# A hybrid attention and recurrent layer on one core: weights as the stationary operand for the columns of the recurrent branch

## The reference

```
h    = rms_norm(x) * norm_w * (1 + scale) + shift      # scale, shift from silu(c) @ w_ada
proj = h @ w_in                                        # q | k | v | z_a | f | x_r | z_r
att  = forgetting_attention(q, k, v, f)                # 16 heads of 128
y_a  = (att * silu(z_a)) @ w_br_attn
xc   = causal_conv4(x_r) + conv_b                      # per channel, over tokens
r, i = sigmoid(xc_block @ w_rg_a + b), sigmoid(xc_block @ w_rg_x + b)   # 16 blocks of 128
a    = exp(-8 * r * softplus(-lru_lambda))
hr_t = a_t * hr_(t-1) + sqrt(1 - a_t^2) * (i_t * xc_t) # a scan over tokens
y_r  = (hr * silu(z_r)) @ w_br_rnn
g    = sigmoid(h @ w_gate + b_gate)                    # g_a | g_r
y    = x + gate_res * ((g_a * y_a + g_r * y_r) @ w_out)
```

## Time and profile before

| | |
|---|---|
| median of three runs | 2623.95 us (2623.81 to 2624.01) |
| the profiled execution's own time | 2624.72 us |
| its span, first to last instruction | 2622.9 us |
| PE busy (matmuls) | 2579.7 us, 98% of the span |
| PEld busy (weight loads) | 2138.8 us, 82% |
| DVE, ACT, POOL busy | 73%, 47%, 1% |
| granted TensorE clock, mean | 0.997 of full |
| DMA | 266 GB/s on average |

### The profile page before, as it was taken

One profiled execution on the slowest core, in us unless ns is written; L12 is line 12 of the kernel. 1 busy time (PEld: TensorE's weight loads), 2 busy tenths in 40 slices (PEclk: granted clock), 3 DMA queues, 4 the chain that ended last, 5 costly groups with the idle time before them and its releaser, 6 DMA issues.

```text
span 2622.9 us, 30908 instructions
## 1 busy us (share of the span) xinstructions
PE 2579.7 (98%) x11668; PEld 2138.8 (82%) x11668; DVE 1906.0 (73%) x1885; ACT 1231.7 (47%) x1436; POOL 18.1 (1%) x32
## 2 busy tenths in 40 slices
PE   4999999999999999999999999999999999999999
PEld 4888888888888888888888888888888888888887
DVE  6889999899888566665666666668787878754544
ACT  4554333433343466654566555554444444433333
POOL 0000000000000000000000000000000000000000
PEclk8999999999999999999999999999999999999999
DMA  9999999999998566445666666679998989667675
GB/s 373 345 333 348 326 356 337 338 351 335 347 343 290 168 195 185 131 143 163 197 194 198 198 198 198 197 268 356 311 352 312 351 312 350 215 209 225 210 225 173
DMA packets 351128, 698.77 MB, mean 266 GB/s; under 512 B 26338, under 2 KB 30724, under 8 KB 350724
## 3 DMA queue, kind: packets, MB, share of 16 engines
q1 hardware_dynamic: 350608, 696.69, 79.3%
q10 hardware_dynamic: 372, 0.12, 0.0%
HBM read 692.45 MB, written 4.19 MB: 266 GB/s over the span
## 4 chain that ended last, share of the span: by engine, by line
PE 97%; DMA 1%; DVE 1%; issue 0%; ACT 0%; SPq 0%; DVEq 0%; ACTq 0%
PE ps_acc L1110 31%; PE ps_acc L1112 31%; PE ps_acc L1118 31%; DMA ada_first<-in_w_ada 1%; PE ps_t L1192 1%; PE ps_t L1237 1%; PE ps_c L1158 0%; DVE acc L743 0%; PE ps_t L1190 0%; PE ps_t L1229 0%; PE ps_t L1181 0%; PE ps_t L1246 0%; PE ps_c L1200 0%; PE ps_t L1272 0%; PE ps_d L1209 0%
## 5 line engine op out<-in xcount | busy, mean ns | idle before, releaser
L539 ACT ACTIVATE w_hi<-land 128x1024 fp32r<-128x1024 f32 x896 | 950.6, 1061 | 1301.4 <-PE ps_acc L1112 1059.8
L726 DVE TENSOR_TENSOR w_lo<-land,w_hi 128x1024 fp32r<-128x1024 f32 x896 | 1094.2, 1222 | 634.0 <-ACT w_hi L539 633.5
L1110 PE MATMUL ps_acc<-w_hi,h_hi 128*128 128x512 f32 x3068 | 1203.8, 392 | 0.0
L1112 PE MATMUL ps_acc<-w_hi,h_lo 128*128 128x512 f32 x3068 | 1195.3, 390 | 0.0
L1118 PE MATMUL ps_acc<-w_lo,h_hi 128*128 128x512 f32 x3068 | 821.0, 389 | 0.0
L1118 PEld LDWEIGHTS ps_acc<-w_lo,h_hi 128*128 128x128 f32 x3068 | 575.6, 188 | 121.7 <-DVE w_lo L726 1.3
L1112 PEld LDWEIGHTS ps_acc<-w_hi,h_lo 128*128 128x128 f32 x3068 | 576.6, 188 | 118.9
L1110 PEld LDWEIGHTS ps_acc<-w_hi,h_hi 128*128 128x128 f32 x3068 | 576.6, 188 | 118.7
L743 DVE SCALAR_TENSOR_TENSOR acc<-ada_ring,cvec,acc 128x1024 f32<-128x1024 f32 x217 | 277.4, 1279 | 4.1 <-DMA ada_ring<-in_w_ada 3.8
L1008 DVE SCALAR_TENSOR_TENSOR racc<-res_land,cvec,racc 128x1024 f32<-128x1024 f32 x124 | 158.6, 1279 | 0.4 <-DMA res_land<-in_w_ada 0.4
L861 DVE TENSOR_TENSOR store<-ps_acc,store 128x1024 f32<-128x1024 f32 x89 | 108.5, 1219 | 13.1 <-PE ps_acc L1118 12.9
(11 more groups left out here) (200 smaller groups left out, 1042.2 us busy)
## 6 DMA issues: line engine op xcount, KB each, us to landing
land<-in_w_in SPq DMA_DIRECT2D x384, 512.0 KB, 4.7
land<-in_w_gate SPq DMA_DIRECT2D x256, 512.0 KB, 4.5
ada_ring<-in_w_ada SPq DMA_DIRECT2D x224, 512.0 KB, 5.8
res_land<-in_w_ada SPq DMA_DIRECT2D x128, 512.0 KB, 7.7
land<-in_w_out SPq DMA_DIRECT2D x128, 512.0 KB, 4.5
land<-in_w_br_attn SPq DMA_DIRECT2D x64, 512.0 KB, 4.2
land<-in_w_br_rnn SPq DMA_DIRECT2D x64, 512.0 KB, 5.9
ada_first<-in_w_ada SPq DMA_DIRECT2D x32, 512.0 KB, 12.2
```

The costliest lines, as they stand in the source:

```text
L539: act.activation(w_hi[:, n % PARTS], land[:, n % LAND], ACT.Copy).then_inc(hi_rdy, 1)
L726: dve.tensor_tensor(w_lo[:, n % PARTS], land[:, n % LAND], w_hi[:, n % PARTS].bitcast(F32), ALU.subtract).then_inc(split_done, 1)
L1110: pe.matmul(ps_acc[:, par, t], l_hi(kk, t), w_hi[:, n % PARTS, kk], start=first and kk == 0, stop=False)
L1112: ins = pe.matmul(ps_acc[:, par, t], l_lo(kk, t), w_hi[:, n % PARTS, kk], start=False, stop=False)
```

## The change

For the 8 column blocks of x_r and z_r (128 of the 384 units of w_in) the operands change places. A new function says which jobs these are, and a new one issues their matmuls: 128 columns of the weights are stationary, and all 256 tokens of `h_hi` or `h_lo` move. The result has channels on the partitions and tokens along the row, so the four transposes of each recurrent block go, with the bank `rt` and the semaphore `xz_t`; ACT and DVE read x_r and z_r from `store`. The wait for `hh_rdy` moves from PE to ACT, since `xc` is now written without waiting for PE.

```
+def by_channel(j):
+    kind, index, *_ = JOBS[j]
+    return kind == "w" and COLUMNS[index[0]][0] in ("xr", "zr")
...
-        rt = tq
+        def acc_blocks(j):
+            par = j % ACCS
+            if by_channel(j):
+                return ps_acc[:, par].rearrange("p t c -> p (t c)").rearrange("p (b t d) -> p b t d", b=BPJ, t=NT)
+            return ps_acc[:, par].rearrange("p t (b d) -> p b t d", d=P)
...
             def rg_step(off, n):            # ACT
                 if off == 2:
-                    act.wait_ge(xz_t, n + 1)
-                    act.activation(xc[:], rt[:, 0:2].rearrange("p a b -> p (a b)"), ACT.Identity,
+                    if n:
+                        act.wait_ge(hh_rdy, n)
+                    else:
+                        act.wait_ge(acc_free, FREED[FINAL["xr", 3]][1])
+                    act.activation(xc[:], store[:, XR_BLK + n].rearrange("p t d -> p (t d)"), ACT.Identity,
...
                         st.did(dve.scalar_tensor_tensor(
-                            xc[:, back:], rt[:, 0:2].rearrange("p a b -> p (a b)")[:, :SEQ - back],
+                            xc[:, back:], store[:, XR_BLK + n].rearrange("p t d -> p (t d)")[:, :SEQ - back],
...
-                    st.did(dve.tensor_tensor(hh[:], rt[:, 2:4].rearrange("p a b -> p (a b)"), hh[:],
+                    st.did(dve.tensor_tensor(hh[:], store[:, ZR_BLK + n].rearrange("p t d -> p (t d)"), hh[:],
...
+                if by_channel(j):
+                    unit_by_channel(n, par, k, first, last)
+                    return
...
+            def unit_by_channel(n, par, k, first, last):
+                out = ps_acc[:, par].rearrange("p t c -> p (t c)")
+                for kk in range(UK):
+                    r_hi, r_lo = (a[:, k * UK + kk].rearrange("p t d -> p (t d)") for a in (h_hi, h_lo))
+                    for b in range(BPJ):
+                        w = w_hi[:, n % PARTS, kk, b * P:(b + 1) * P]
+
+                        pe.matmul(out[:, b * SEQ:(b + 1) * SEQ], w, r_hi, start=first and kk == 0 and b % 2 == 0,
+                                  stop=False, skip_group_check=True)
+                        ins = pe.matmul(out[:, b * SEQ:(b + 1) * SEQ], w, r_lo, start=False, stop=False,
+                                        skip_group_check=True)
+                ins.then_inc(hi_used, 1)
+                pe.wait_ge(split_done, n + 1)
+                for kk in range(UK):
+                    r_hi = h_hi[:, k * UK + kk].rearrange("p t d -> p (t d)")
+                    for b in range(BPJ):
+                        ins = pe.matmul(out[:, b * SEQ:(b + 1) * SEQ], w_lo[:, n % PARTS, kk, b * P:(b + 1) * P], r_hi,
+                                        start=False, stop=last and kk == UK - 1, skip_group_check=True)
+                ins.then_inc(unit_done, 1)
...
             def rg_step(off, n):            # PE
-                if off == 0:
-                    if n:
-                        pe.wait_ge(hh_rdy, n)
-                    else:
-                        pe.wait_ge(acc_free, FREED[FINAL["xr", 3]][1])
-                    for s in range(2):
-                        for t in range(NT):
-                            ins = pe.transpose(rt[:, s * 2 + t], store[:, (XR_BLK, ZR_BLK)[s] + n, t], ident[:])
-                    ins.then_inc(xz_t, 1)
```

More of the change, by code:

```diff
@@ L369, in build @@
         bias_in, gate_rdy, gate_used = sem("bias_in"), sem("gate_rdy"), sem("gate_used")
-        wrg_in, xz_t, tap0, xc_rdy, rg_done = (sem("wrg_in"), sem("xz_t"), sem("tap0"), sem("xc_rdy"),
+        wrg_in, tap0, xc_rdy, rg_done = (sem("wrg_in"), sem("tap0"), sem("xc_rdy"),
                                                sem("rg_done"))
@@ L650, in _ @@
                     b0 = COLUMNS[JOBS[j][1][0]][2]
-                    act.activation(store[:, b0:b0 + BPJ].rearrange("p b t d -> p t b d"),
-                                   ps_acc[:, j % ACCS].rearrange("p t (b d) -> p t b d", d=P), ACT.Copy
-                                   ).then_inc(acc_copied, 1)
+                    part, view = store[:, b0:b0 + BPJ], acc_blocks(j)
+                    if not by_channel(j):
+                        part, view = (v.rearrange("p b t d -> p t b d") for v in (part, view))
+                    act.activation(part, view, ACT.Copy).then_inc(acc_copied, 1)
                 for g in range(1, GROUPS):
@@ L691, in _ @@
                             b0 = COLUMNS[JOBS[j][1][0]][2]
-                            act.activation(store[:, b0:b0 + BPJ].rearrange("p b t d -> p t b d"),
-                                           ps_acc[:, j % ACCS].rearrange("p t (b d) -> p t b d", d=P),
-                                           ACT.Sigmoid).then_inc(z_sig, 1)
+                            part, view = store[:, b0:b0 + BPJ], acc_blocks(j)
+                            if not by_channel(j):
+                                part, view = (v.rearrange("p b t d -> p t b d") for v in (part, view))
+                            act.activation(part, view, ACT.Sigmoid).then_inc(z_sig, 1)
                 for step, h in HEADS_AT.get(n - 2, []):
@@ L853, in empty @@
                     part = store[:, b0:b0 + BPJ]
-                    view = ps_acc[:, par].rearrange("p t (b d) -> p b t d", d=P)
+                    view = acc_blocks(j)
                     jobs = [i for i in range(j) if JOBS[i][0] == "w" and JOBS[i][1][0] == index[0]]
@@ L887, in silu_mul @@
                 part = store[:, b0:b0 + BPJ]
-                dve.tensor_tensor(part, ps_acc[:, j % ACCS].rearrange("p t (b d) -> p b t d", d=P), part,
-                                  ALU.mult).then_inc(acc_free, 1)
+                dve.tensor_tensor(part, acc_blocks(j), part, ALU.mult).then_inc(acc_free, 1)
             def f_step(off):
```

## The result

| | before | after |
|---|---|---|
| median (6 runs each) | 2623.98 us (2623.81 to 2624.36) | 2634.78 us (2634.42 to 2635.40) |
| the profiled execution | 2624.72 us | 2635.03 us |
| ratio of the times, 95% interval | | 1.0041 (1.0031 to 1.0052) |

The change makes the kernel 10.8 us slower, where the prediction had 6.6 us less and held everything above 2630 us for unlikely. The time is within 1.4 us of rival 1 (2636.2 us). The page after, as in the earlier trace rows: its first line, engines busy, and the chain by engine.

What follows compares the result with a forecast made beforehand. PE was taken to bound the kernel. Transposes -7.7, matmul pitch +0.8 and edges +0.3 gave -6.6 us: profiled 2624.72 becomes 2618.1, as a median 2617.4 us (-0.25%), range 2615.8 to 2630.

Steps and rivals of the forecast that it cites:

- rival 1: Changed w_in units: the full weight load slows each 256-column matmul to 119.7 ns; sum +12.2, 2636.2 us; chance 0.13.
- What bounds the kernel: In the w_in units and recurrent blocks nothing but PE sets the time; it is busy 979.38 of 980 us and 490.00 of 490.
- The gain: Recurrent blocks: dropping 64 transposes at 16 places, 0.48 us each, takes 7.7 us off PE.
- edits that cost nothing: ACT and DVE work off the path: plain adds about as long as strided, taps from SBUF some 3 us less DVE.
- the price of a matmul of 256 columns: Changed w_in units: 113.6 ns each, taken from f_product's fp32r run with 16 stationary columns; 3072 matmuls add 0.8 us.
- the edges: Where the kinds of unit change place, seven stretches were priced at 0.05 us each, 0.3 us.
- the exact half: f_product's 113.3 ns pitch is half the long matmul's 226.7, taken as evidence against a load-dependent part.
- Rival 2: Changed units: a fixed cost of 3 ns per matmul adds 4.6 us; sum -2.8, 2621.2 us, same; chance 0.10.
- Rival 3: Changed units: the slow pitch behind short matmuls stays, 117.0 ns; sum +4.0, 2628.0 us, same; chance 0.16.
- Rival 5: Recurrent blocks: no gain from the transposes, PE waits for `xc_rdy` or a weight split instead; 2624 us; chance 0.04.
- Rival 4: Changed units: the weight load is not hidden, 224 ns a matmul; +341 us, 2957 us; chance 0.05.
- What would show it: Profile signs: new matmuls 113 to 114 ns apart; wrong if 80 to 1060 us grows by more than 3 us.

Runs made afterwards that it cites:

- e_no_turns: The kernel before without the 64 transposes, its recurrent branch computed from untransposed values; 2616.67 us against 2624.28, ratio 0.9970.
- e_pitch: The kernel before with rows of 48 independent matmuls of various operand widths added behind its last unit; 2751.1 us, only its pitches count.
- e_pitch2: The kernel before with ten more rows of 48 independent matmuls, other types and widths, behind its last unit; 2713.26 us, only its pitches count.

## Why the prediction was wrong

**What bounds the kernel** was read rightly. PE set the time in both stretches before and after, and no new wait came in either. That nothing but PE set the time was a little too strong: of the 20.5 us that the settled pitch adds, 0.8 went into waits that PE had before, one of them the 0.62 us that the text's own 979.38 of 980 shows.

**The gain** of 7.7 us (16 places of 0.48 us) is measured: 7.65 us between the unit starts, 7.6 us in e_no_turns.

The **edits that cost nothing** cost nothing, as PE's idle time in the two stretches is none. One size in them was off, though. The groups of DVE after, the counterparts of L861 and L964 in the earlier trace rows:

```profile
L878 DVE TENSOR_TENSOR store<-ps_acc,store 128x1024 f32<-128x1024 f32 x89 | 108.4, 1218 | 16.2 <-PE ps_acc L1137 9.4 <-PE ps_acc L1157 6.6
...
L980 DVE SCALAR_TENSOR_TENSOR xc<-store,prm,xc 128x254 f32<-128x254 f32 x16 | 7.8, 485 | 0.6
```

The adds, strided and plain ones together, take 1218 ns as forecast. The taps read SBUF and still take 485 ns, where 412 was expected after L976, so the 3 us less of DVE did not come. L976 has neither the offset into the tile nor `prm` as scalar, and was no fit row for the tap. It cost nothing here, since PE covers it.

**The step that failed** is the price of a matmul of 256 columns, 113.6 ns, "since it is the nearest in type, shape and accumulation". It is 120.0 ns. The sum had 0.8 + 0.3 us for it and for the edges; in its place stand 20.5 us by the settled pitch, of which 18.0 arrived. (The edges are next to nothing: the first unit of a stretch adds 0.10 us and the old-kind one behind it 0.08, together the 0.16 of one unit and 0.02 more.) The prediction named the one thing that f_product's row lacks, the full load, and then took its price all the same. Two arguments carried that. The first was that loads can follow each other every 111 ns and so fit under 113. This is true (the floor of 111.7 ns in e_pitch), but it bounds the pitch only from below: it says what the loads allow, not what a matmul under a full load costs. The second was that the exact half would otherwise be a coincidence. It was one: e_pitch splits the two numbers into 106.7 + 6.7 and 213.3 + 13.4.

**The rivals.** Rival 1 was the case, with 119.7 ns for the pitch and 2636.2 us for the time, against 120.0 and 2634.8. Its arithmetic came from the one other row at hand, the plain float32 matmuls, whose pitch of 0.214 us it took for the time of the columns alone. That was in part luck: those matmuls have full loads too, and they show no such surplus (in e_pitch 215.9 ns against 213.3, with a small load 215.8), so they don't bear out that the difference belongs to the load; they only gave nearly the right time for the columns. That its total came so near is luck too: with 120.0 ns its own sum gives 2637.0 us, and the change stayed under that by most of the 2.5 us above. Its chance of 0.13 was too small for a case that no row spoke against but a coincidence: two rows with different loads cannot tell load from columns, so neither reading deserved four times the other. Its words are right for the full load only; e_pitch's 16 x 512 row (18.4 ns of surplus) shows that a small load is no sure way round it. Rival 2 had the right form, a constant in each matmul, but 3 ns for it where 13.3 are measured, and it did not tie it to the load. (Its mark of 116 ns doesn't fit its own sum either: 4.6 us over 3072 matmuls is a pitch of 114.8.) Rival 3 falls: the pitch is 120.0 and not 117.0, and it is 120 as well in a row of independent matmuls. Rival 5 falls, for no new wait came in that stretch. Rival 4 falls too: 120 ns holds a load of 188 ns and a stream. Of rival 3 a piece is real, on the other side: long matmuls are slow for some ten pitches behind short ones, and the change lost less than 20.5 us because its short ones aren't (1.5 of the 2.5 us).

**What would show it** did: the text gave 119 as rival 1's mark and 3 us of growth in the first stretch as the point at which the prediction is wrong.

**Open.** Why fp32r pays 13.3 ns where bf16 pays 2.5, and why 16 x 512 pays 18.4, no run here tells, nor what law the widths of 272, 288, 448 and 504 follow. The difference of 20.5 and 18.0 us is read from unit starts and waits to all but 0.2 us, and no kernel was run for it alone.

## What to carry to other kernels

Where PE is the bound, price a matmul by a row of the same type, the same moving width and the same size of weight load; if one of the three differs, the price is open by a whole surplus, and a ratio that comes out neat is no evidence. In fp32r, halving the moving width under a full load costs 6.7 ns per half on this chip (120.0 against 113.3), so a change of operands that saves transposes has to save more than that times its matmuls: here 64 transposes (7.7 us) against 3072 halves (18.0). When a surplus turns up in one place, ask which other matmuls pay it: 10.9 of the 13.3 ns in every long fp32r matmul were worth 32 us in 256 of the 896 units, at the price of shorter operands. And PE's busy share of 100% does not say that PE never waits: read the distances between starts.

## What the runs showed of the hardware

- Full weight loads of 128 columns follow each other at 111.7 ns at best in fp32r: 128, 192 and 240 moving columns cost about the same (111.7 to 112.0 ns), and 256 cost 120.0. With 16 or 64 stationary columns, 128 moving ones cost 60.0.
- The stationary operand's columns count for the surplus and its rows don't: 64 rows by 128 columns under 256 moving columns cost 120.0 ns, 128 rows by 64 columns 113.3.
- The surplus is no simple function of load and width: 16 stationary columns pay 6.7 ns at 256 moving ones and 18.4 at 512, and under a full load it is 11.9 ns at 272 columns, 13.3 at 496 and 16.7 at 504 (e_pitch, e_pitch2).
- Under a full load bf16 pays 2.5 ns in its place (215.8 ns for 512 columns), and plain float32 2.6 (215.9 ns for a record of 256 columns, which takes the time of 512).
- A load's record in fp32r grows by 0.83 ns a column over some 81 ns: 95, 108, 134, 161, 174 and 188 ns for 16, 32, 64, 96, 112 and 128 stationary columns. The pitch does not follow it.
- Behind a stretch of shorter matmuls, the first ten or so of 512 columns start 224 to 236 ns apart instead of 226.7, some 0.05 us in all. Those of 256 columns behind the same heads are at 119 at once.
